# One product-key expert step, two layers: the planned order of selection, gathered rows and one-hots

## The chip, the core and the metric

The kernel runs on one core of a Trainium2 chip. The metric is the device time of one execution in microseconds (us). TensorE (PE), VectorE (DVE), ScalarE (ACT), GpSimd (POOL) and SyncE (SP) each run their own queue in order; the queues meet at semaphores. A transfer (DMA) is issued from the queue of SP, ACT or POOL.

## The reference, cut to what matters

Two trunk layers over 640 tokens (128 context, 512 latent; five blocks of 128). Each layer has a mixer and then an expert retrieval, `peer`. The mixers and the norms are not touched here.

```python
def peer(h, w_q, sub_keys, u_tab, v_tab):             # T = 640 tokens, D = 1024
    q = (x @ w_q).reshape(T, 8, 2, 128)               # 8 heads, two sides
    scores = einsum('thsd,hskd->thsk', q, sub_keys)   # 128 keys a side
    s, i = top_k(scores, 16)                          # per side
    cand = s[:, :, 0, :, None] + s[:, :, 1, None, :]  # 16 x 16 sums
    top, sel = top_k(cand, 16); idx = take(i0 * 128 + i1, sel)
    g = softmax(top)                                  # 16 experts of 16384 for each head and token
    a = gelu(einsum('td,thkd->thk', x, u_tab[idx]))
    return einsum('thk,thkd->td', g * a, v_tab[idx])
```

## The kernel before

The expert step of a layer has three stretches. The first two share one planned order; the third follows it.

**Two ways to an expert's output.** For the first two blocks of tokens ("gathered blocks", `GB = 2`) the rows of both tables are fetched by index: a gather moves 128 rows of 4 KB, one for each token. A "dot" (L1484) multiplies a gathered u row with the token and sums it; an "add" (L1519) adds a gathered v row, weighted, to the result. There are `ROWS` = 256 dots and 256 adds; a dot and an add together are called a pair here. For the other three blocks ("dense blocks", `DB = 3`) all 16384 experts are computed: PE multiplies every u row with every token in 128 u jobs (a few tokens, 32 of the third block, go by 32 extra gathered dots, "qdots", L1494), the chosen gates are scattered into a dense gate matrix, and PE multiplies the product with the whole v table (the value stretch). Gates are scattered by matmuls of one-hots: a "hot" is four tokens' one-hots, made by DVE (L1531, L1533) and partly by ACT (the "build" steps), and a scatter is PE's four matmuls of it. There are 96 hots and 96 scatters in a layer.

**Selection.** For each head (`PHEADS = 8`) PE computes two q jobs and five scores (one for each block); DVE then does five "choose" blocks (eight parts each, L1391 to L1419) and a "batch" (13 parts) which turns the picks of all five blocks into indices and gates. Part 0 of the batch subtracts the maximum and lets ACT compute the exponentials; part 10 writes the gathered rows' indices (L1460), releases the gathers and then waits for ACT's exponentials (L1468); parts 11 and 12 finish the gates.

**The order.** `dve_order` writes DVE's queue by hand: the whole first head, then dots from 0 on, each followed (from dot `LAG` = 20 on) by the add that is 20 behind it, and after each of these as much of the remaining work (chooses, batches, hots, qdots: `rest`, by the guessed costs in `CHOOSE`, `BATCH` and beside the kinds) as `each` has paid for. `each` is the cost of all remaining work over `EARLY * TOPK` = 160 pairs. When the rest is done, "weigh" steps (L1560, L1561: gate times activation for one of 32 chunks of the value stretch) follow among the remaining pairs. POOL walks the same list and issues the gathers; each table has a ring of `RING` = 4 buffers, so a gather waits for the dot or add four before it.

`peer_steps_of` writes PE's and ACT's common order: a walk over `dve_order` with a planned clock (1.03 times the guessed cost, from 20 us on) gives a due time for each score, exponential, build and scatter (3 us behind the hot it needs), and the jobs are laid out with what is due put between them, by `COST` (8.9 us for a q job, 4.95 for a u job). The last `LATE` = 4 jobs are kept back until every scatter is placed. DVE may be at most `OHB` = 4 hots ahead of PE's scatters. u weights are loaded two jobs at a time into four slots (`peer_jobs`, `peer_weights`).

**End of the second stretch.** After the last scatter ACT copies it out and stores the last gates to memory (L1158); then SP loads gates for the first chunks (1.5 MB, strided); then DVE weighs chunk 0 and PE starts on the values.

Of the kernel before, what the change touches and what calls it, by code (L numbers as in the profile page):

```python
# [8 lines left out]
BF16 = mybir.dt.bfloat16  # L9
# [55 lines left out]
EARLY = 10  # L65
SPREAD = 28
LATE = 4
# [76 lines left out]
def program(nc, x_in, cond_t, norm_gain, final_gain, ada_w, ada_b, ada_fix_in, ab_w_in, ab_w_out, decays, states,  # L144
# [3 lines left out]
    with ctx:  # L148
# [93 lines left out]
        pair, side_h, which = (bcf[:, 3328 + i * 80:3408 + i * 80].bitcast(BF16).rearrange("p (k c) -> p k c", c=SIDES) for i in range(3))  # L242
# [38 lines left out]
        part_i = small[:, 1360:1520].rearrange("p (k b s) -> p b s k", b=BLOCKS, s=2)  # L281
# [136 lines left out]
        def peer_jobs(l):  # L418

            loads, jobs = [], []  # L420

            def load_of(kind, c, n):
                loads.append((kind, c, len(jobs) + n))
                jobs.extend((kind, c * n + i, len(loads) - 1) for i in range(n))

            for c in range(CHUNKS):
                for q in [n for n, at in enumerate((0, 0, 2, 2, 6, 6, 10, 10)) if at == c]:
                    load_of("q", q, 2)
                for half in range(2):
                    load_of("u", 2 * c + half, 2)  # L430
            return loads, jobs

        CHOOSE = (.58, 1.47, .56, 1.2, .27, .65, .27, .34)
        BATCH = (1.2, .75, .25, 1.5, 1.5, .8, .45, .3, .25, .6, .4, .1, .4)

        def dve_order():

            picks = []
            for h in range(PHEADS):
                picks += [("choose", h, b, i, w) for b in range(BLOCKS) for i, w in enumerate(CHOOSE)]  # L440
                picks += [("batch", h, 0, i, w) for i, w in enumerate(BATCH)]
# [7 lines left out]
            first = len(CHOOSE) * BLOCKS + len(BATCH)  # L449
            order, rest = picks[:first], picks[first:]  # L450
            each, due, pairs, weighed = sum(p[4] for p in rest) / int(EARLY * TOPK), 0.0, 0, 0
            for i in range(ROWS + LAG):
# [6 lines left out]
                due += each  # L459
# [10 lines left out]
        COST = {"q": 8.9, "u": 5.4 * DU / DT}  # L470

        def peer_steps_of(jobs):

            ready, clock, begun = [], 20.0, [0.0] * SCORE_LEAD
            for kind, a, b, i, w in dve_order():
# [5 lines left out]
                clock += 1.03 * w  # L481
# [4 lines left out]
                if kind == "batch" and a == PHEADS - 1 and i == len(BATCH) - 1:  # L486
                    ready += [(clock + 1, "turn", b, 0) for b in ORDER[:-1]]
                    ready += [(clock + 1, "build", ORDER[0], g) for g in range(OHB - 2)]
# [4 lines left out]
                if kind == "hot":  # L493
# [3 lines left out]
                    ready.append((clock + 3, "scatter", a, b))  # L497
# [549 lines left out]
        def _(act):  # L1047
# [49 lines left out]
            def peer(l):  # L1097
# [63 lines left out]
                for kind, a, i in steps:  # L1161
                    if kind == "job":
                        take_job(a)
                    elif kind == "exp":
                        act.wait_ge(top_ready, l * PHEADS + a + 1)
                        f(top_e, top_e, ACT.Exp).then_inc(exp_ready, 1)
# [110 lines left out]
        def _(v):  # L1277
# [101 lines left out]
            def peer(l):  # L1379
# [41 lines left out]
                def batch(h, part):  # L1421
# [4 lines left out]
                    top = top_i.rearrange("p b k -> p (b k)")  # L1426
                    of = lambda t: t.rearrange("p (b k) -> p b k", b=BLOCKS)
                    to = pair.rearrange("p k (b s) -> p b s k", s=2)
                    wide4 = onehot.rearrange("p (a k c) -> p a k c", a=TOPK, k=TOPK)
                    if part == 0:  # L1430
                        v.wait_ge(scores_read, l * BLOCKS * PHEADS + (h + 1) * BLOCKS)
                        v.tensor_tensor(top_e, top_v, top_v[:, :, 0:1].to_broadcast([P, BLOCKS, TOPK]), ALU.subtract)\
                            .then_inc(top_ready, 1)
                        for t, n, op in ((by16, 4, ALU.logical_shift_right), (by4, 2, ALU.logical_shift_right),
                                         (mid2, 12, ALU.bitwise_and), (low2, 3, ALU.bitwise_and)):
                            own.mark(v.tensor_scalar(t, top, n, None, op))
                    elif part == 1:
                        own.mark(v.scalar_tensor_tensor(out=to[:, :, 0, :], in0=of(by4), scalar=float(WIDE * TOPK // NARROW - WIDE),
                                                        in1=of(by16), op0=ALU.subtract, op1=ALU.max))
                        own.mark(v.scalar_tensor_tensor(out=off, in0=top, scalar=float(WIDE * TOPK), in1=mid2, op0=ALU.is_lt, op1=ALU.mult))  # L1440
                        own.mark(v.tensor_copy(side_h.rearrange("p k c -> p (k c)"), small[:, 960:1120].bitcast(U32)))
                    elif part == 2:
                        own.mark(v.tensor_tensor(to[:, :, 1, :], of(off), of(low2), ALU.add))
                    elif part == 3:
                        own.mark(v.tensor_tensor(wide4, pair.unsqueeze(1).to_broadcast([P, TOPK, TOPK, SIDES]),
                                                 which.unsqueeze(2).to_broadcast([P, TOPK, TOPK, SIDES]), ALU.is_equal))
                    elif part == 4:
                        own.mark(v.tensor_tensor(wide4, wide4, side_h.unsqueeze(2).to_broadcast([P, TOPK, TOPK, SIDES]), ALU.mult))
                    elif part <= 8:
                        n = NP * (8 >> part - 5)  # L1450
                        out = onehot[:, 0:n] if part < 8 else small[:, 1360:1520]
                        own.mark(v.tensor_tensor(out, onehot[:, 0:n], onehot[:, n:2 * n], ALU.add))
                    elif part == 9:
                        own.mark(v.tensor_copy(ijg[:, :, 0:2, at], part_i[:, GB:BLOCKS, :, :]))
                        own.mark(v.scalar_tensor_tensor(out=part_i[:, 0:GB, 0, :], in0=part_i[:, 0:GB, 0, :], scalar=float(NKEYS),
                                                        in1=part_i[:, 0:GB, 1, :], op0=ALU.mult, op1=ALU.add))
# [415 lines left out]
```

## Time and profile before

| | us |
|---|---|
| median of 3 runs (4048.28 to 4056.04) | 4049.79 |
| the profiled execution | 4056.96 |
| its span, first to last instruction | 4055.1 |
| layer 0: first q job to last scatter | 555.84 to 1444.7 |
| layer 0: value stretch | 1469.58 to 2131.0 |
| layer 1: first q job, start of values | 2470.22, 3379.93 |

PE is busy for 3866.5 us of the span (95%), DVE for 2628.7 (65%), POOL for 1447.8 (36%), ACT for 688.7 (17%). Times in the views are counted from the first instruction. Matmuls overlap, so the length of a PE piece is read from its start to the start of the next. A matmul of 32-bit numbers shows as two records: a u job is 16 records, a q job 32, a scatter 8, a score 4.

### The profile page before, as it was taken

The numbers are of one execution on the slowest core, as the hardware profiler recorded it, in microseconds if no ns is written. First come the engines' busy times: TensorE is split into PE (matmuls) and PEld (weight loads), VectorE is DVE, ScalarE is ACT, GpSimd is POOL, SyncE is SP. The second block draws the span as 40 slices with busy tenths as digits, with TensorE's granted clock in tenths as the row PEclk, the third lists the DMA queues.
The fourth block names the chain that finished last, engine by engine and source line by source line (L and its number), as shares of the span: only waits on it lengthen the run. The fifth ranks groups of instructions, "written<-read, shape, count | busy, mean of one in ns | idle before, by whom it ended". The sixth has DMA issues, their size and how long they took to land.

```text
span 4055.1 us, 36430 instructions
## 1 busy us (share of the span) xinstructions
PE 3866.5 (95%) x12776; PEld 2211.7 (55%) x12776; DVE 2628.7 (65%) x5808; ACT 688.7 (17%) x1591; POOL 1447.8 (36%) x1180
## 2 busy tenths in 40 slices
PE   8999889999988989999998999999999899999998
PEld 1555556666656744444445545666666674444443
DVE  2682558998777955454445944998977894445444
ACT  1111011111334620000001221111143460000000
POOL 0110003554556634444320000455545663434331
PEclk9999899999989999999999999999999999999999
DMA  9452037999999999999972101899999999999994
GB/s 333 160 195 83 8 128 286 331 334 342 342 379 396 405 365 353 341 355 358 329 259 83 42 31 46 313 333 325 343 351 384 410 404 345 363 352 345 352 326 168
DMA packets 377653, 1155.57 MB, mean 285 GB/s; under 512 B 28720, under 2 KB 163360, under 8 KB 346360
## 3 DMA queue, kind: packets, MB, share of 16 engines
q0 software_dynamic: 170016, 618.96, 41.5%
q1 hardware_dynamic: 198368, 483.93, 32.7%
q10 hardware_dynamic: 9088, 50.37, 3.0%
q8 instruction: 102, 1.67, 0.2%
q14 instruction: 79, 0.65, 0.0%
HBM read 1055.68 MB, written 97.40 MB: 284 GB/s over the span
## 4 chain that ended last, share of the span: by engine, by line
PE 75%; DMA 10%; DVE 10%; POOL 3%; issue 1%; ACT 1%; SPq 0%; DVEq 0%; POOLq 0%
PE bank L744 74%; DMA ring<-in_peer_v,work 4%; POOL ring L696 3%; DMA ring<-in_peer_u,q_t 3%; DVE diag L1519 2%; DVE ring L1484 1%; DVE bc L1533 1%; DMA ring<-in_peer_u,work 1%; DVE bc L1531 1%; DVE ring L1651 1%; DMA bc<-peer_gates 1%; DMA ring<-in_ada_w 1%; DVE ring L1494 0%; DMA peer_gates<-work 0%; ACT hT L1050 0%
## 5 line engine op out<-in xcount | busy, mean ns | idle before, releaser
L744 PE MATMUL bank<-hT,ring 128*128 128x352 f32 (+3 forms) x5696 | 1691.8, 456 | 3.3 <-ACT hT L1050 3.3
L744 PEld LDWEIGHTS bank<-hT,ring 128*128 128x128 f32 x5696 | 1058.7, 193 | 560.7 <-issue 83.0
L696 POOL DMA_INDIRECT ring<-in_peer_u,work x512 | 753.3, 1471 | 1360.2 <-DVE ring L1484 1075.0
L744 PE MATMUL bank<-ring,work 128*128 128x512 f32 x2016 | 868.8, 592 | 0.0
L1519 DVE SCALAR_TENSOR_TENSOR diag<-ring,work,diag 128x1024 f32<-128x1024 f32 x508 | 652.5, 1285 | 96.5 <-DMA ring<-in_peer_v,work 84.4
L696 POOL DMA_INDIRECT ring<-in_peer_v,work x512 | 557.2, 1088 | 296.0 <-issue 155.2
L1484 DVE SCALAR_TENSOR_TENSOR ring<-ring,work 128x1024 f32<-128x1024 f32 x512 | 623.9, 1219 | 49.2 <-DMA ring<-in_peer_u,work 48.9
L744 PEld LDWEIGHTS bank<-ring,work 128*128 128x128 f32 x2016 | 383.0, 190 | 482.2 <-issue 482.2
L1050 ACT ACTIVATE work<-bank 128x352 f32<-128x352 f32 (+3 forms) x528 | 274.6, 522 | 1560.3 <-PE bank L744 1513.9
L744 PE MATMUL bank<-work 128*128 128x512 f32 x1056 | 461.4, 597 | 9.7 <-DVE work L1561 9.7
L1560 DVE COPY work<-bc 128x128 f32<-128x128 f32 x64 | 14.5, 227 | 663.7 <-DMA work<-peer_acts 443.7
L744 PE MATMUL bank<-ring,hT 128*128 128x384 f32 (+1 forms) x960 | 353.4, 525 | 8.5 <-ACT hT L1050 8.5
L744 PEld LDWEIGHTS bank<-work 128*128 128x128 f32 x1056 | 202.2, 192 | 265.2 <-issue 265.2
L744 PE MATMUL bank<-bc 128*128 128x128 f32 x1536 | 211.6, 288 | 74.1 <-DVE bc L1533 65.7
L744 PEld LDWEIGHTS bank<-ring,hT 128*128 128x128 f32 x960 | 180.3, 191 | 171.3 <-issue 83.9
L744 PEld LDWEIGHTS bank<-bc 128*128 128x128 f32 x1536 | 199.2, 200 | 107.9 <-DVE bc L1533 78.6
L1050 ACT ACTIVATE work<-work 128x16 f32<-128x16 f32 (+3 forms) x49 | 14.2, 304 | 1115.1 <-DVE ring L1484 1102.3
L1050 ACT ACTIVATE bc<-work,small 128x128 f32<-128x128 f32 x352 | 152.8, 483 | 0.0
L1788 DVE SCALAR_TENSOR_TENSOR work<-work,small 128x670 f32<-128x670 f32 x180 | 149.4, 905 | 0.0
L1533 DVE TENSOR_TENSOR bc<-small,keep 128x512 f32<-128x512 f32 x192 | 130.3, 679 | 0.0
L1531 DVE TENSOR_SCALAR bc<-keep,small 128x128 f32<-128x128 f32 x416 | 122.2, 340 | 11.7 <-ACT small L1050 10.8
L744 PE MATMUL bank<-ring,stat 128*2 128x512 f32 x240 | 107.7, 603 | 15.4 <-DMA ring<-in_ada_w 15.4
(178 smaller groups left out, 2077.1 us busy)
## 6 DMA issues: line engine op xcount, KB each, us to landing
ring<-in_peer_ut SPq DMA_DIRECT2D x128, 1024.0 KB, 8.4
ring<-in_peer_vt SPq DMA_DIRECT2D x42, 2048.0 KB, 9.9
peer_gates<-work ACTq DMA_DIRECT2D x48, 1024.0 KB, 8.7
bc<-peer_gates SPq DMA_DIRECT2D x32, 1536.0 KB, 22.3
work<-in_peer_vt SPq DMA_DIRECT2D x22, 2048.0 KB, 10.3
peer_acts<-work SPq DMA_DIRECT2D x60, 704.0 KB, 6.3
work<-peer_acts SPq DMA_DIRECT2D x60, 704.0 KB, 13.9
ring<-in_ada_w SPq DMA_DIRECT2D x12, 2048.0 KB, 14.4
```

The costliest lines, as they stand in the source:

```text
L696: nc.gpsimd.indirect_dma_start(row, None, table, bass.IndirectOffsetOnAxis(ap=at, axis=0)).then_inc(s, 16)
L744: return nc.tensor.matmul(out, lhsT, rhs, start=start, stop=stop, **kw)
L1050: return nc.scalar.activation(out, in_, func, **kw)
L1484: v.scalar_tensor_tensor(out=row, in0=row, scalar=1.0, in1=h_tok[:, n % GB, :], op0=ALU.mult, op1=ALU.mult, accum_out=dots[:, n % 2, k:k + ...
L1519: v.scalar_tensor_tensor(out=a, in0=row, scalar=wgt[:, n % 2, k:k + 1], in1=a, op0=ALU.mult, op1=ALU.add).then_inc(v_free, 1)
L1531: v.tensor_scalar(oh[:, n % OHB, 0, o, :], iota, ijg_t[:, b, 0, t0 + o:t0 + o + 1], ijg_t[:, b, 2, t0 + o:t0 + o + 1], ALU.is_equal, ALU.mult)
L1533: v.tensor_tensor(oh[:, n % OHB, 1, :, :], ijg_t[:, b, 1, t0:t0 + OH].unsqueeze(2).to_broadcast([P, OH, NKEYS]), iota.unsqueeze(1).to_broa ...
L1560: v.tensor_copy(w[:, :, 0:skip, :], g[:, :, 0:skip, :])
L1651: ins = v.scalar_tensor_tensor(out=a, in0=w, scalar=by, in1=a, op0=ALU.mult, op1=ALU.add)
L1788: ins = v.scalar_tensor_tensor(out=y_conv[:, f, :], in0=src, scalar=w, in1=y_conv[:, f, :], op0=ALU.mult, op1=ALU.add)
```

## The change

Rates, paces and a split of the first head; no engine gets another kind of work.

- `EARLY = 10` for all remaining work becomes two rates: selection is paid over 6.25 x 16 = 100 pairs and the hots and qdots over 3 x 16 = 48.
- `GROUPS`: the first head is selected in two groups, first the two gathered blocks alone and later the three dense ones; the other heads in one group as before. So there are nine batches; `batch` works on blocks b0 to b1 and writes gathered indices only in groups that hold the gathered blocks.
- The last three parts of a batch (sum of the exponentials, reciprocal, gates) become `share`, which follows the first choose block of the next group.
- The planned order of PE and ACT uses other paces (0.957 during selection, 1.1 after), other job costs, scatters 8 us behind their hot instead of 3, `LATE` = 6, and scores of the first head one job earlier. The q weights are loaded a half chunk apart.

```diff
-EARLY = 10
+EARLY_CHOICE, EARLY = 6.25, 9.25
-LATE = 4
+LATE = 6
+BEHIND = 8
+PACE = {True: 0.957, False: 1.1}
+BEGIN = 20.0
...
-                for q in [n for n, at in enumerate((0, 0, 2, 2, 6, 6, 10, 10)) if at == c]:
-                    load_of("q", q, 2)
                 for half in range(2):
+                    for q in [n for n, at in enumerate((0, 1, 4, 5, 12, 13, 20, 21)) if at == 2 * c + half]:
+                        load_of("q", q, 2)
                     load_of("u", 2 * c + half, 2)
...
-        BATCH = (1.2, .75, .25, 1.5, 1.5, .8, .45, .3, .25, .6, .4, .1, .4)
+        BATCH = (1.2, .75, .25, 1.5, 1.5, .8, .45, .3, .25, .6, .4)
+        SHARE = (.25, .2, .4)
+        GROUPS = [(0, 0, GB), (0, GB, BLOCKS)] + [(h, 0, BLOCKS) for h in range(1, PHEADS)]
+        NG = len(GROUPS)
...
-            for h in range(PHEADS):
-                picks += [("choose", h, b, i, w) for b in range(BLOCKS) for i, w in enumerate(CHOOSE)]
-                picks += [("batch", h, 0, i, w) for i, w in enumerate(BATCH)]
+            shared = lambda s: [("share", s, 0, i, w) for i, w in enumerate(SHARE)]
+            for s, (h, b0, b1) in enumerate(GROUPS):
+                for b in range(b0, b1):
+                    picks += [("choose", h, b, i, w) for i, w in enumerate(CHOOSE)]
+                    if s and b == b0:
+                        picks += shared(s - 1)
+                picks += [("batch", s, 0, i, w * (.3 + .7 * (b1 - b0) / BLOCKS)) for i, w in enumerate(BATCH)]
+            picks += shared(NG - 1)
...
-            first = len(CHOOSE) * BLOCKS + len(BATCH)
+            first = len(CHOOSE) * GB + len(BATCH)
             order, rest = picks[:first], picks[first:]
-            each, due, pairs, weighed = sum(p[4] for p in rest) / int(EARLY * TOPK), 0.0, 0, 0
+            work = lambda kinds: sum(p[4] for p in rest if p[0] in kinds)
+            chosen, placed = work(("choose", "batch", "share")), work(("hot", "qdot", "qweight"))
+            choice_rate, hot_rate = chosen / (EARLY_CHOICE * TOPK), placed / ((EARLY - EARLY_CHOICE) * TOPK)
...
-                due += each
+                due += (choice_rate if rest and rest[0][0] in ("choose", "batch", "share") else hot_rate)
...
-        COST = {"q": 8.9, "u": 5.4 * DU / DT}
+        COST = {"q": 9.15, "u": 5.16 * DU / DT}
...
-                clock += 1.03 * w
+                choosing = choosing and kind != "hot"
+                clock += PACE[choosing] * w
...
-                    ready.append((clock + 3, "scatter", a, b))
+                    ready.append((clock + BEHIND, "scatter", a, b))
...
-                return ready[0][1] != "score" or q_at[2 * ready[0][2] + 1] + 2 <= n
+                return ready[0][1] != "score" or q_at[2 * ready[0][2] + 1] + (2 if ready[0][2] else 1) <= n
...
-                    now += {"score": .6, "turn": .5, "scatter": 1.1}.get(step[0], 0)
+                    now += {"score": .45, "turn": .5, "scatter": 1.08}.get(step[0], 0)
...
-                        v.wait_ge(exp_ready, l * PHEADS + h + 1)
-                        own.mark(v.tensor_reduce(top_s, top_e, AX.X, ALU.add))
+                def share(s, part):
+                    if part == 0:
+                        v.wait_ge(exp_ready, l * NG + s + 1)
+                        own.mark(v.tensor_reduce(top_s[:, b0:b1], top_e[:, b0:b1], AX.X, ALU.add))
```

## Rows read from the trace of the kernel before

**Rows 1.** Chain of waits, end of layer 0's second stretch: start us, us, what.

```profile
1442.65 2.09 PE bank L744 x8
...
1445.38 7.37 DMA peer_gates<-work
1452.83 14.64 DMA bc<-peer_gates
...
1469.58 661.42 PE bank L744 x1536
```

**Rows 2.** Busy time by stretch: selection, one-hots in two parts, values; layer 1's first one-hot part.

```profile
core 0: us, PE busy (x) PEld busy (x) DVE busy (x) ACT busy (x) POOL busy (x), PEclk, DMA share, GB/s
555.80:1063.30 507.50, 507.46 (x1856) 341.03 (x1857) 424.67 (x1496) 69.63 (x119) 223.89 (x178) 1.00 0.81 297
...
1085.70:1292.90 207.20, 181.38 (x736) 125.38 (x735) 154.03 (x262) 77.09 (x202) 124.23 (x99) 0.93 0.99 391
1292.90:1441.90 149.00, 138.55 (x722) 105.39 (x720) 137.06 (x275) 99.43 (x261) 94.05 (x63) 0.98 1.01 404
1469.60:2131.00 661.40, 661.38 (x1536) 292.49 (x1536) 306.17 (x371) 5.89 (x14) 245.88 (x203) 1.00 0.92 332
...
3000.40:3206.80 206.40, 180.31 (x736) 124.96 (x735) 153.96 (x262) 76.78 (x202) 118.88 (x101) 0.93 1.00 399
```

**Rows 3.** PE's waits from 1060 to 1480: who waited for whom, us, times, longest.

```profile
PE bank L744 <- DVE bc L1533: 33.5, 15, 4.9
PE bank L744 <- DVE work L1561: 5.1, 1, 5.1
```

**Rows 4.** PE in order of time: start us, us, instructions, idle before.

```profile
585.00 8.78 PE L744 MATMUL bank<-hT,ring 128*128 128x320 f32 x32
593.62 0.61 PE L744 MATMUL bank<-bc,work 128*128 128x128 f32 x4
594.06 4.90 PE L744 MATMUL bank<-hT,ring 128*128 128x352 f32 x16
...
1135.15 1.05 PE L744 MATMUL bank<-bc 128*128 128x128 f32 x8
1136.04 4.90 PE L744 MATMUL bank<-hT,ring 128*128 128x352 f32 x16
1140.77 1.05 PE L744 MATMUL bank<-bc 128*128 128x128 f32 x8
...
1313.33 1.95 PE L744 MATMUL bank<-bc 128*128 128x128 f32 x16
...
1316.41 4.90 PE L744 MATMUL bank<-hT,ring 128*128 128x352 f32 x16
...
1433.28 1.13 PE L744 MATMUL bank<-bc 128*128 128x128 f32 x8 [0.70 <-issue]
1435.12 1.13 PE L744 MATMUL bank<-bc 128*128 128x128 f32 x8 [0.70 <-DVE bc L1533]
```

**Rows 5.** DVE's groups, 555.8 to 1469.6: shapes, count | busy us, mean ns | idle before.

```profile
L1484 DVE SCALAR_TENSOR_TENSOR ring<-ring,work 128x1024 f32<-128x1024 f32 x165 | 201.1, 1219 | 23.4 <-DMA ring<-in_peer_u,work 23.3
L1519 DVE SCALAR_TENSOR_TENSOR diag<-ring,work,diag 128x1024 f32<-128x1024 f32 x143 | 183.1, 1281 | 35.9 <-DMA ring<-in_peer_v,work 33.0 <-issue 2.4
```

**Rows 6.** Waits from 624 to 1060, DVE for the exponentials.

```profile
DVE small L1468 <- ACT small L1050: 32.6, 5, 9.5
```

**Rows 7.** DMA queues from 1085.7 to 1292.9, the gathers': packets, MB, share.

```profile
q0 software_dynamic: 14056, 51.16, 64.1%
```

**Rows 8.** Waits from 1470 to 2160, DVE before its weigh steps.

```profile
DVE work L1560 <- DMA work<-peer_acts: 231.2, 15, 17.1
DVE work L1560 <- PE bank L744: 79.8, 15, 14.4
```

**Rows 9.** POOL in order of time, first gather of layer 0.

```profile
614.96 1.01 POOL L696 DMA_INDIRECT ring<-in_peer_u,work  x1 [83.97 <-DVE work L1460]
```

**Rows 10.** The hots' L1533 alone in one-hot part 1: length, DVE busy and count.

```profile
1085.70:1292.90 207.20, 21.80 (x32) 0.93 0.99 391
```

More of the change, by code:

```diff
@@ L241, in program @@
         onehot = bcf[:, 2048:2048 + TOPK * NP // 2].bitcast(BF16)
-        pair, side_h, which = (bcf[:, 3328 + i * 80:3408 + i * 80].bitcast(BF16).rearrange("p (k c) -> p k c", c=SIDES) for i in range(3))
+        pair, side_h, which = (bcf[:, 3328 + i * 80:3408 + i * 80].bitcast(BF16) for i in range(3))
         by16, by4, low2, mid2, off = (bcf[:, 3568 + i * 80:3648 + i * 80].bitcast(U32) for i in range(5))
@@ L485, in peer_steps_of @@
                     ready.append((clock + 3, "gelu", a // TOPK, 0))
-                if kind == "batch" and a == PHEADS - 1 and i == len(BATCH) - 1:
+                if kind == "share" and a == NG - 1 and i == len(SHARE) - 1:
                     ready += [(clock + 1, "turn", b, 0) for b in ORDER[:-1]]
@@ L1419, in choose, with batch @@
                         own.mark(v.max_index(top_i[:, b, 8:16], top_v[:, b, 8:16], cand_left))
-                def batch(h, part):
+                def batch(s, part):
+                    h, b0, b1 = GROUPS[s]
+                    n, lo, heads_c = b1 - b0, GB - b0, 2 * (b1 - b0)
                     at = slice(h * TOPK, (h + 1) * TOPK)
@@ L1444, in batch @@
                     elif part == 3:
-                        own.mark(v.tensor_tensor(wide4, pair.unsqueeze(1).to_broadcast([P, TOPK, TOPK, SIDES]),
-                                                 which.unsqueeze(2).to_broadcast([P, TOPK, TOPK, SIDES]), ALU.is_equal))
+                        own.mark(v.tensor_tensor(wide4, in_rows(pair).unsqueeze(1).to_broadcast(wide_shape),
+                                                 which.rearrange("p (k c) -> p k c", c=SIDES)[:, :, 0:heads_c].unsqueeze(2).to_broadcast(wide_shape),
+                                                 ALU.is_equal))
@@ L1447, in batch @@
                     elif part == 4:
-                        own.mark(v.tensor_tensor(wide4, wide4, side_h.unsqueeze(2).to_broadcast([P, TOPK, TOPK, SIDES]), ALU.mult))
+                        own.mark(v.tensor_tensor(wide4, wide4, in_rows(side_h).unsqueeze(2).to_broadcast(wide_shape), ALU.mult))
                     elif part <= 8:
-                        n = NP * (8 >> part - 5)
-                        out = onehot[:, 0:n] if part < 8 else small[:, 1360:1520]
-                        own.mark(v.tensor_tensor(out, onehot[:, 0:n], onehot[:, n:2 * n], ALU.add))
+                        m = TOPK * heads_c * (8 >> part - 5)
@@ L1453, in batch @@
+                        out = onehot[:, 0:m] if part < 8 else part_i[:, 0:m]
+                        own.mark(v.tensor_tensor(out, onehot[:, 0:m], onehot[:, m:2 * m], ALU.add))
                     elif part == 9:
-                        own.mark(v.tensor_copy(ijg[:, :, 0:2, at], part_i[:, GB:BLOCKS, :, :]))
-                        own.mark(v.scalar_tensor_tensor(out=part_i[:, 0:GB, 0, :], in0=part_i[:, 0:GB, 0, :], scalar=float(NKEYS),
-                                                        in1=part_i[:, 0:GB, 1, :], op0=ALU.mult, op1=ALU.add))
@@ L1578, in peer @@
                 v.wait_ge(h_ready[2 * l + 1], BLOCKS)
-                own.mark(v.tensor_copy(which, iota[:, 0:TOPK].unsqueeze(2).to_broadcast([P, TOPK, SIDES])))
+                own.mark(v.tensor_copy(which.rearrange("p (k c) -> p k c", c=SIDES), iota[:, 0:TOPK].unsqueeze(2).to_broadcast([P, TOPK, SIDES])))
                 for kind, a, b, i, _ in dve_order():
@@ L1584, in peer @@
                         batch(a, i)
+                    elif kind == "share":
+                        share(a, i)
                     elif kind == "hot":
```

86 lines of the change are left out of this document (54 added, 32 removed).

## The prediction

> **What bounds the kernel now.** I read the busy times by stretch first, then the chain of waits, then who made PE wait, then PE in order of time. In layer 0 selection keeps PE busy for 507.46 of 507.5 us at full clock, and the value stretch for 661.38 of 661.4 [rows 2]: there the time is PE's own work. Only the one-hots leave a gap. In their first part, the 32 hots that carry the qdots [rows 10], PE is busy for 181.4 of 207.2 us at a granted clock of 0.93, and the DMA engines are full: 391 GB/s, 399 in layer 1, 404 in the part after [rows 2]. PE waits 33.5 us for DVE's hots [rows 3], and DVE for rows, 23.3 and 33.0 us [rows 5]. So the chain there is: gathers, dots and adds, the hot queued behind them on DVE, the scatter. At the end comes a tail: last scatter from 1442.65, gates stored 7.37, gates loaded 14.64, weigh, values from 1469.58 [rows 1]. The four jobs kept back cover it all but 5.1 us [rows 3].
>
> What PE would need without waits is a sum. From start to start a u job takes 4.73, a scatter 0.89, a q job 8.62, a score 0.44 [rows 4]. Selection before: 74 u, 16 q and 40 scores, 350.0 + 137.9 + 17.6 = 505.5; measured 507.5, so 2.0 for the start. All of it (128 u, 16 q, 40 scores, 96 scatters, three transposes of 0.45) is 847.7 + 2.0 = 849.7 us. From 555.84 to 1469.58 it took 913.7. The 64 us between the two are all that a better order can win in a layer.
>
> **The change, part by part.** The order is worked out from the formulas. Before, one rate paid for everything: 427.8 of guessed cost over 160 pairs, 2.67 a pair. Now selection gets 272.4 over 100 (2.72) and hots and qdots 181.4 over 48 (3.78). The first hot then stands behind dot 101 (93 before), the ninth behind 104 (98), the 41st behind 127 (131), the last behind 149 (161). So the hots have 48 pairs among them instead of 68, and 12 pairs go to the value stretch; selection takes 8 more.
>
> *Selection* costs PE nothing that I can find. DVE was busy for 424.7 us there [rows 2]. Eight more dots at 1.22 and adds at 1.28 [rows 5] are 20 us; the second batch of head 0 repeats some fifteen short instructions, 3 us estimated. The first score is done 18 us after PE's start (two q jobs and no third), at 574.6, so DVE ends near 574.6 + 448 + 10 (the first gather on its way) = 1033. PE asks for the gates when its sum reaches the transposes: now 75 u jobs stand ahead, 512.3 us, so 1068; I add 2 for the first score, which waits for ACT to take its q job, and for an exponential now and then at which ACT waits for DVE with jobs queued behind: 1070. There are 37 us to spare; even if DVE still waited the 32.6 us for exponentials [rows 6] that `share` should take off, 4 would be left. That saving and the earlier first gather (POOL waited 84 us for it [rows 9]) are therefore worth 0 by themselves: PE hides them. Moved q loads: every job still finds two loads ahead of it; 0.
>
> *One-hots, first eight.* Two u jobs now stand ahead of the first scatter. The ninth hot needs the fifth scatter done (four buffers): two transposes, four u jobs, five scatters, 24.3 us, so it starts at 1094 (1085.7 before).
>
> *One-hots with qdots.* From the 9th to the 41st hot there were 33 dots, 32 qdots and 33 adds, 98 gathers of 0.52 MB: the queue's 51.16 MB [rows 7]. Now it is 23, 32 and 23: 78, 40.7 MB. The other traffic was 81.0 - 51.2 = 29.8 MB; with 27 u jobs for 29 and the same 32 scatters I take 28. At 391 GB/s 68.7 MB take 176 us. PE's own sum here is 27 x 4.73 + 32 x 0.89 = 156, so DMA still sets the end, by less than before. Bounds: if the gathers alone count, 207.2 x 78/98 = 165; if nothing but PE does, 156; if a hot costs as much as now, 207. I take 176: bytes over a rate that three rows show within 4%. The 41st hot starts at 1270; its scatter ends at 1272.
>
> The Trainium skill (DMA: Bandwidth & Descriptors, Specifications) gives some 358 GB/s as a core's memory limit and 435 as the fabric's ceiling. By 358 this part would take 192 us and the sum lose 16 us a layer; the 391, 399 and 404 measured here are above it, so it is no limit in this trace. By 435 it would take 158, which is the first rival; no stretch read here holds that rate.
>
> *The other one-hots.* DVE was busy for 137.1 of 149 us [rows 2]; eight pairs fewer at 2.50 leave 117. PE needs 15 u jobs, 55 scatters and a transpose: 120.4. Three scatters in a row take 3.08, not 2.67, and the last run goes at 1.84 apiece [rows 4]; nine threes, a four and a run of 14 ahead of the last jobs (10 before) add 3.7 + 1 + 13.3. That is 138 us, and PE bounds it now: last scatter done at 1411.
>
> *The tail.* Six jobs are kept back: 28.4 us, over the tail's 24.9 (1444.7 to 1469.6 [rows 1]). So the 5.1 us wait goes; ACT's take of the last job costs about 1. Values start at 1440, where they started at 1469.6: 29.5 us. In layer 1 the first part was served at 399 GB/s, so it needs 172 us; that layer went from first job to values in 909.7 us and now in 881: 29.
>
> *Value stretch.* Twelve pairs more: 30 us of DVE, which was busy for 306 of 661 [rows 2] and waited 79.8 us for PE and 231 for stored activations [rows 8]; they go into that idle time. 12.5 MB more make 351 GB/s of 332, below what the one-hots carried. I cost it at 0. Were that cover gone, it would be 12.5 MB at 332 GB/s, 38 us a layer.
>
> **The sum**: the profiled execution took 4056.96, less 58 gives 3999. It lies 7.2 above the median of the runs, so the forecast for the median is 3991.
>
> **The rivals.** First, *PE alone*: DVE may run four hots ahead, DMA holds a rate nearer its peaks, and the qdot part fits into PE's 156 us. Then the 41st scatter ends 14 us earlier: 44 us a layer, 3963. For it speaks that four hots, some 19 us at PE's pace, nearly cover the 20 us by which the gathers are late; against it that 68.7 MB in 156 us are 440 GB/s, and no stretch read here went above 404.
>
> Second, *half the gain*: scatters are planned 1.1 times DVE's guessed cost and 8 us behind, and the qdot part is planned at 162 us where I expect 176. If latency and not bytes holds the u gathers (a gather waits for the dot four before), or a PE wait lowers the clock as it did (0.93 [rows 2]), 190 us are possible: 14 us less in each layer, 4020.
>
> Third, *nothing comes of it*: the 32 hots still take 207 us, since qdots, not pairs, hold DVE. The sum is then 31 us a layer worse and the time 4050 to 4055. Against it: 20 of 98 gathers are gone.
>
> Fourth, *slower*: the value stretch pays. If weighs there come after gathers that no longer land in time, PE waits in the one stretch where it never did. It decides from the point where a weigh is later than the product before it, so more than 20 us of lead have to go; its price is the 38 us above, against 29 won: 9 us a layer lost, 4068. The Trainium skill's 358 GB/s (DMA: Bandwidth & Descriptors, Specifications) would be nearly reached by 351, yet not passed, so by that rule too the stretch stays as it is. Against it speaks that DVE waits for PE there already [rows 8].
>
> That the change does not do what it says (the gates late, so the transposes wait at 1070) needs DVE to lose 37 us in selection; I count it with the third.
>
> **How the numbers follow.** My case 0.58 (3978 to 4008), PE alone 0.16, half 0.13, nothing 0.06, slower 0.07. A difference of 0.2% (8 us) is about what a measurement of this kernel can tell. Faster by more: 0.58 + 0.16 + 0.13 = 0.87; within: 0.06; slower: 0.07. The range takes in the first three: 3955 to 4032.
>
> **What would show it.** The first transposes at about 1070 with no wait of PE before them; the 41st hot near 1270, with 170 to 180 us for the 32 before it at 385 to 405 GB/s; PE's waits for DVE (33.5 us [rows 3]) down to about half; the last scatter near 1411, then six jobs and values with under 1.5 us between; the value stretch still 661 us. DVE's wait for exponentials gone, and no gain to be seen from it before 1063. Wrong would be: PE idle in selection, ACT waiting for DVE for more than one job's 4.7 us, or a value stretch over 665 us.

## The result, and the profile after

The changed kernel takes 3988 us where the kernel before, timed beside it, takes 4051: a ratio of 0.9835 (95% interval 0.9821 to 0.9849), 63 us less. The forecast was 3991, within 3955 to 4032. The profiled execution took 3988.73 us with a span of 3986.9, which is 68.2 less than the span before.

The busy times by stretch answer [rows 2]: selection, the one-hots with qdots (9th to 41st hot), the other one-hots, the values of layer 0, then the qdot part of layer 1. Columns: stretch, length, busy time of each engine with its instructions, granted clock, DMA share, GB/s.

```profile
553.50:1068.10 514.60, 513.71 (x1872) 344.70 (x1873) 445.32 (x1538) 72.97 (x124) 243.15 (x193) 0.99 0.86 310
1092.90:1269.60 176.70, 166.53 (x724) 116.57 (x722) 129.78 (x231) 78.89 (x200) 89.65 (x78) 0.99 0.99 387
1269.60:1401.30 131.70, 122.95 (x683) 95.84 (x683) 118.44 (x251) 97.85 (x256) 62.84 (x46) 1.00 0.99 386
1433.85:2093.30 659.45, 659.45 (x1536) 291.76 (x1536) 339.80 (x409) 6.11 (x15) 277.39 (x227) 1.00 0.95 351
2971.30:3144.30 173.00, 164.29 (x712) 114.99 (x711) 129.75 (x231) 78.93 (x200) 93.67 (x79) 0.99 1.00 390
```

The qdot part went from 207.2 to 176.7 us and from 206.4 to 173.0, with the DMA engines as full as before; the rest of the one-hots from 149.0 to 131.7. The value stretch carries 351 GB/s where it carried 332, and PE is busy through all of it.

From the first job to the values, both kernels in layer 0 (first the kernel before, from 555.8):

```profile
555.80:1469.60 913.80, 871.32 (x3498) 602.78 (x3498) 749.26 (x2090) 265.86 (x634) 462.78 (x354) 0.98 0.89 337
```

```profile
553.50:1433.85 880.35, 859.22 (x3497) 595.37 (x3497) 722.30 (x2069) 271.86 (x636) 414.13 (x330) 0.99 0.90 336
```

The 33.45 us gained in this layer are 21.35 us of idle PE (42.48 before, 21.13 now) and 12.1 us by which the same PE work got shorter (871.3 to 859.2). The last section shows that most of the 12.1 is PE's clock.

PE's waits for DVE's hots answer [rows 3]; here from 1060 to 1440 (who waited for whom, us, times, longest). They went from 33.5 to 14.8 us, and the wait for the first weigh (5.1 us) is gone.

```profile
PE bank L759 <- DVE bc L1573: 14.8, 11, 4.8
PE bank L759 <- issue: 2.6, 3, 1.2
PE bank L759 <- ACT work L1065: 2.1, 3, 0.8
```

The end of the second stretch answers [rows 1] (PE in order of time: start, us, instructions, idle before). Behind the last scatter stand six jobs (96 records), then the values with 0.55 us between.

```profile
1402.08 1.99 PE L759 MATMUL bank<-bc 128*128 128x128 f32 x8 [1.43 <-DVE bc L1573]
1403.87 29.43 PE L759 MATMUL bank<-hT,ring 128*128 128x352 f32 x96
1433.85 6.70 PE L759 MATMUL bank<-work 128*128 128x512 f32 x15 [0.55 <-ACT work L1065]
```

Two executions had a lower granted clock and are not compared: one of the changed kernel (5332.9 us, mean clock 0.718) and the profiled one of the kernel with `LATE` 4 (4642.2 us, 0.826).

Where the span's 68.2 us went: 2.4 ahead of layer 0's first job, 33.4 from there to its values (913.7 to 880.4), 1.5 from there to layer 1's first job, 28.3 in layer 1 (909.7 to 881.4), 2.6 behind it. 61.7 of them lie in the two planned stretches. The 1.5 and the 2.6 come from the value stretches, which are 1.9 and 2.5 us shorter (661.4 and 662.0 before, 659.5 now in both layers). Before, PE waited 5.1 and 4.6 us for the first weigh, and the values then began at about half the clock; now they begin at the full one. The rows are the first 4.4 us of layer 0's values before, then their first 6.1 us now:

```profile
1469.60:1474.00 4.40, 4.40 (x6) 1.98 (x7) 1.39 (x1) 0.00 (x0) 0.00 (x0) 0.55 0.98 417
```

```profile
1433.90:1440.00 6.10, 6.10 (x15) 2.75 (x16) 1.69 (x2) 0.00 (x0) 0.00 (x0) 1.00 0.95 336
```

### The profile page after: what moved, and what is told of

It is laid out like the page before. It is cut to its first block, busy times and chain, and to the rows that moved or that the text cites. A ratio compares the mean times of both kernels' runs of the same rounds, so it can differ in the third digit from the quotient of the medians.

```text
span 3986.9 us, 36490 instructions
## 1 busy us (share of the span) xinstructions
PE 3840.1 (96%) x12776; PEld 2195.3 (55%) x12776; DVE 2642.8 (66%) x5842; ACT 701.6 (18%) x1597; POOL 1413.5 (35%) x1180
## 4 chain that ended last, share of the span: by engine, by line
PE 84%; DVE 7%; DMA 7%; ACT 1%; issue 1%; POOL 1%; ACTq 0%; DVEq 0%; SPq 0%
PE bank L759 83%; DMA ring<-in_peer_u,q_t 3%; DMA ring<-in_peer_v,work 2%; DVE ring L1693 1%; DMA ring<-in_peer_u,work 1%; DVE diag L1559 1%; DVE ring L1534 1%; DVE bc L1573 1%; DMA ring<-in_ada_w 1%; POOL ring L711 1%; DVE ring L1524 1%; DVE bc L1571 0%; DMA peer_gates<-work 0%; ACT work L1065 0%; ACT hT L1065 0%
## 5 line engine op out<-in xcount | busy, mean ns | idle before, releaser
L711 POOL DMA_INDIRECT ring<-in_peer_u,work x512 | 730.3, 1426 | 1339.5 <-DVE ring L1524 1042.3
L759 PE MATMUL bank<-bc 128*128 128x128 f32 x1536 | 197.9, 281 | 38.4 <-DVE bc L1573 27.6
L759 PEld LDWEIGHTS bank<-bc 128*128 128x128 f32 x1536 | 190.7, 195 | 65.6 <-DVE bc L1573 40.0
L1065 ACT ACTIVATE work<-keep,small 128x128 f32<-128x128 f32 x352 | 120.8, 393 | 30.8 <-PE bank L759 14.2
## 6 DMA issues: line engine op xcount, KB each, us to landing
ring<-in_ada_w SPq DMA_DIRECT2D x12, 2048.0 KB, 14.4
```

The source lines that it names most:

```text
L711: nc.gpsimd.indirect_dma_start(row, None, table, bass.IndirectOffsetOnAxis(ap=at, axis=0)).then_inc(s, 16)
L759: return nc.tensor.matmul(out, lhsT, rhs, start=start, stop=stop, **kw)
L1065: return nc.scalar.activation(out, in_, func, **kw)
```

## The experiments

Between sessions one kernel's time moves by more than within one. The changed kernel was timed again beside the last three kernels:

> The changed kernel itself, unaltered, timed beside the next three. Theory and rivals alike expect 3988 us within 12, and a ratio to the kernel before of 0.9835 within 0.003. It tells whether the 3977 to 3979 us of the two kernels without the split and with the shares beside their loads differ from it.

It took 3975.6 us (3969.1 to 3978.2), 12.8 less than in the first session. Its ratio to the kernel before is 0.9823 (0.9809 to 0.9836), and it agrees with the first. So kernels timed in different sessions are compared below by their ratios, and by stretches of their traces. The traces of one kernel differ too: the second one of the changed kernel has 876.1 and 870.3 us from first job to values, where the first has 880.4 and 881.4. A difference of up to some 10 us a layer between two traces is therefore not a finding by itself.

**The pairs put back, the rest of the change kept.**

```diff
-EARLY_CHOICE, EARLY = 6.25, 9.25
+EARLY_CHOICE, EARLY = 6.25, 10.5
-PACE = {True: 0.957, False: 1.1}
+PACE = {True: 0.957, False: .95}
```

> The changed kernel with 20 pairs put back among the hots (68 instead of 48) and the planner's pace set so that PE's order around the scatters is the same to the step where it matters. Theory: 98 gathers and 27 u jobs between the 9th and the 41st hot, 79 MB, 203 us at 391 GB/s instead of 177; the rest as slow as before (147 us); values start about 922 us after the first q job, and the time is 4060 to 4080, no better than before. Rival (the new selection and the new paces give the gain): at most 4020.

With 68 pairs a pace of 0.95 gives PE nearly the order that 1.1 gives with 48: no scatter moves past more than one job, and six jobs follow the last. It took 4066.6 us, a ratio of 1.0035 (1.0021 to 1.0050). The qdot part is back at its old length (first row, columns as above), and PE waits 42.8 us for hots. From first job to values it takes 921.9 and 919.8 us.

```profile
1091.30:1298.70 207.40, 176.97 (x722) 122.80 (x720) 154.13 (x263) 80.90 (x204) 123.33 (x98) 0.92 0.99 381
...
PE bank L759 <- DVE bc L1573: 42.8, 16, 6.9
```

The gain hangs on the pairs: without them the split, the shares and the changed plan give nothing.

**The rates alone**, put into the kernel before; PE's order is planned from them by the old paces.

```diff
-EARLY = 10
+EARLY_CHOICE, EARLY = 5.8125, 8.8125
...
-            each, due, pairs, weighed = sum(p[4] for p in rest) / int(EARLY * TOPK), 0.0, 0, 0
+            work = lambda kinds: sum(p[4] for p in rest if p[0] in kinds)
+            chosen, placed = work(("choose", "batch")), work(("hot", "qdot", "qweight"))
+            choice_rate, hot_rate = chosen / (EARLY_CHOICE * TOPK), placed / ((EARLY - EARLY_CHOICE) * TOPK)
+            due, pairs, weighed = 0.0, 0, 0
...
-                due += each
+                due += (choice_rate if rest and rest[0][0] in ("choose", "batch") else hot_rate)
```

> The kernel before with nothing changed but the two rates: selection over 93 pairs as it was, hots and qdots over 48. No split of the first head, no share, the old paces, LATE 4. Theory (the gain is the gathers taken out of the one-hots): the 9th to the 41st hot hold 80 gathers (41.8 MB) and 24 u jobs, some 68 MB, so 173 us at 391 GB/s instead of 207; values start about 885 us after the first q job (913.7 before, 880.4 changed), and the time is about 3995 (3985 to 4005). Rival (the split of the first head, the share parts and the paces carry it): 4030 or more.

It took 4027.9 us, a ratio of 0.9945 (0.9926 to 0.9963). That is a miss of the theory, and close to its rival's 4030. What the theory said of DVE holds: the qdot part took 176.2 and 173.1 us, and the last scatter was done 850.1 us after the first job (850.6 in the changed kernel). But eleven jobs stand behind that scatter:

```profile
1400.68 1.13 PE L747 MATMUL bank<-bc 128*128 128x128 f32 x8 [0.17 <-issue]
1401.65 52.23 PE L747 MATMUL bank<-hT,ring 128*128 128x352 f32 x176
1454.44 5.85 PE L747 MATMUL bank<-work 128*128 128x512 f32 x13 [0.55 <-ACT work L1053]
...
PE bank L747 <- DVE bc L1536: 21.7, 12, 5.1
PE bank L747 <- issue: 8.9, 19, 2.1
```

The old plan counts on hots earlier than they come, so PE stood at its scatters with jobs behind them that it could have done. 52 us of jobs, where the tail needs some 25 to 30, put the values 902.7 us after the first job in place of 880.4. DVE's shorter queue is worth its full price only with an order of PE that fits it. All waits listed for PE around the one-hots come to 33.6 us here and to 20.1 in the changed kernel, which is some 13 of these 22 us. PE's own work is 10 us longer (869.2 for 859.2); the clock, worked out as in the last section, is 7 of them.

**The pace alone**, with the changed pairs.

```diff
-PACE = {True: 0.957, False: 1.1}
+PACE = {True: 0.957, False: .95}
```

> The changed kernel with one number other: the planned pace of the hots 0.95 instead of 1.1, so that PE's order puts the 41st scatter 24 us earlier in PE's own sum (677 us after the first job instead of 701) and 11 instead of 6 u jobs behind the last scatter. Theory (the second half of the gain is that PE has jobs to do while DVE waits for rows): DVE's hots come when they came, 41st about 716 us and last about 848 us after the first job, PE waits for them with the jobs still ahead of it, and 11 jobs follow: values at about 901 us instead of 880, 20 us a layer, 4028 (4018 to 4036). Rival (the order of PE does not matter as long as DVE sets the end; what the run with the rates alone lacked was the split, share or LATE): 3988 within 10.

It took 4009.0 us, a ratio of 0.9905 (0.9889 to 0.9922), which is under the theory's band. The direction holds, and the size is smaller than the 40 us that were expected: 28 or 33 us by the ratios (0.9835 and 0.9823 for the changed kernel). From first job to values it takes 890.6 and 891.6 us, 10.2 more in each layer than in the first trace of the changed kernel, and 14.5 and 21.3 more than in the second. Again eleven jobs follow the last scatter, but in layer 0 this scatter comes 12.6 us sooner than in the first trace (838.0 us after the first job). The expectation held the hots' times fixed, and they came sooner: 3.0 us of the 12.6 lie ahead of the qdot part, 6.5 in it and 3.1 behind it. The row of the qdot part, then the u weights' queue (packets, MB, share) in it, here and in the changed kernel:

```profile
1090.90:1261.10 170.20, 147.79 (x639) 105.02 (x638) 129.07 (x232) 77.23 (x197) 93.23 (x80) 0.94 0.99 380
```

```profile
q1 hardware_dynamic: 2448, 15.86, 22.3%
```

```profile
q1 hardware_dynamic: 3024, 19.73, 27.4%
```

With jobs moved out of the part their weights go too: 64.7 MB in place of 68.4. At the changed kernel's 387 GB/s they would take 167 us, and they took 170.2. That the length is bytes over rate stands; the bytes are a choice of the order as well.

**Bytes or latency.** A u load brings the weights of two jobs. From the 45th load on only the first job's weights are loaded, and the second job multiplies what its half of the slot held before (the activations are then not the reference's); every gather stays.

```diff
-                        sp.dma_start(load_slot[n % 4], peer_ut[l, c // 2][:, c % 2 * 2048:(c % 2 + 1) * 2048]).then_inc(load_in[n % 4], 16)
+                        cols = 1024 if c >= 44 else 2048
+                        sp.dma_start(load_slot[n % 4][:, 0:cols], peer_ut[l, c // 2][:, c % 2 * 2048:c % 2 * 2048 + cols]).then_inc(load_in[n % 4], 16)
```

> The changed kernel with only half of the bytes of each u load from the 45th load of u on (the second job of a load multiplies what its half of the slot held before), so the activations are not the reference's; every step and every wait stays. Theory (bytes over a rate bound the hots with qdots): 68.4 MB become 61, 158 us at 387 GB/s, which is PE's own 156; values start some 16 us earlier in each layer, 3957 (3945 to 3965). Rival (the ring: a u gather waits for the dot four before it, so 55 u gathers at 3.2 us each): 174 us or more as before and at most 8 us gained in all, 3980 or more.

It took 3957.2 us, a ratio of 0.9768 (0.9751 to 0.9784). The qdot part carries 61.5 MB in place of 68.4 and takes 162.1 us, with the same 32 hots and the same gathers, and PE is now busy through all of it:

```profile
1094.70:1256.80 162.10, 161.97 (x715) 114.60 (x714) 129.07 (x232) 78.73 (x200) 94.87 (x78) 1.00 0.99 379
...
PE bank L760 <- DVE bc L1574: 3.3, 3, 1.4
```

So bytes set the end in the changed kernel, and not the four buffers of a ring at a fixed time for each gather, with which the rival's 174 us or more would have stayed. The gathers did land sooner with fewer bytes beside them (those of the qdots after 9.4 us at the median, for 10.9), so a landing time that grows with the load is part of the same limit and is not told apart from it here.

**The split of the first head, and the shares.** Each is undone alone.

```diff
-        GROUPS = [(0, 0, GB), (0, GB, BLOCKS)] + [(h, 0, BLOCKS) for h in range(1, PHEADS)]
+        GROUPS = [(h, 0, BLOCKS) for h in range(PHEADS)]
...
-            first = len(CHOOSE) * GB + len(BATCH)
+            first = len(CHOOSE) * BLOCKS + len(BATCH)
```

> The changed kernel with the first head selected in one group again. Theory (PE hides the earlier first gather): no change from the changed kernel, 3988, within 6 us. Rival (selection on DVE needs the earlier start to be done by the transposes): DVE is done some 13 us after the point where PE asks, in each layer, and the time is 4005 to 4015.

```diff
-                    if s and b == b0:
-                        picks += shared(s - 1)
...
-            picks += shared(NG - 1)
+                picks += shared(s)
...
-            first = len(CHOOSE) * GB + len(BATCH)
+            first = len(CHOOSE) * GB + len(BATCH) + len(SHARE)
```

> The changed kernel with the share parts straight behind their batch. Theory (4 us would be left even with the waits for exponentials): 3988, within 6 us. Rival: in the changed kernel DVE was done with selection only 6.5 us before PE asked for the transposes, so 10 to 25 us more of waits push the transposes back by up to 20 us a layer: 4000 to 4025.

They took 3977.3 us, a ratio of 0.9814 (0.9794 to 0.9835), and 3979.1 us, a ratio of 0.9821 (0.9801 to 0.9842). The changed kernel's two ratios are 0.9835 and 0.9823. Neither part is worth anything that these runs can tell. With the shares at once DVE waits 33.0 us for exponentials in selection, and PE does not notice: its first transposes come at 1067.9 us, 514.6 after the first job as in the changed kernel.

```profile
DVE small L1502 <- ACT small L1063: 33.0, 7, 8.1
```

**Fewer jobs kept back.**

```diff
-LATE = 6
+LATE = 4
```

> The changed kernel with four jobs planned behind the last scatter in place of its six; nothing else of PE's order moves by more than two places. Theory: the stretch from the last scatter to the values is set by the last products (24.9 us after the last scatter before the change, 29.8 behind it), four jobs fill 18.9 us of it, PE then stands some 6 us each layer and the stretch is 25 us in place of 29.8; the two jobs taken away lie earlier, where PE waits 14.8 us for one-hots, and take some of that: within 10 us of the changed kernel. Rival: what follows the last scatter is pure addition, and each job taken from there gains its 4.7 us, twice a layer: 19 us less, 3969.

It took 3985.2 us, a ratio of 0.9842 (0.9827 to 0.9857), beside 3975.6 and 0.9823 of the changed kernel on the same chip: 10 us more. The two ranges (3982.1 to 3988.8, and 3969.1 to 3978.2) do not overlap, while the intervals of the ratios do. The rival's 19 us less are excluded; the jobs behind the last scatter do cover a tail. That PE's wait before the values is where the 10 us sit was expected, but no trace that can be compared shows it.

**More pairs to the values: 8, 16 and 32.** The first has only the rate changed, `EARLY` 8.75; the second has

```diff
-EARLY_CHOICE, EARLY = 6.25, 9.25
+EARLY_CHOICE, EARLY = 6.25, 8.25
-PACE = {True: 0.957, False: 1.1}
+PACE = {True: 0.957, False: 1.2}
```

> The changed kernel with hots and qdots over 40 pairs instead of 48 (8 pairs more in the value stretch). By the theory of bytes the 9th to the 41st hot hold 72 gathers and 25 u jobs, 64 MB, 166 us; the long run of scatters at the end is gone from PE's order; 7 jobs follow the last scatter: values start 10 to 17 us earlier in each layer, 3955 to 3970, and the value stretch stays at 659.5 us with some 364 GB/s. Rival (the value stretch pays for them): 8.4 MB at 351 GB/s, 24 us a layer, 4000 or more.

> The changed kernel with hots and qdots over 32 pairs (16 more in the value stretch) and the planned pace of the hots 1.2, so that 6 jobs follow the last scatter. By the theory 62 gathers and 25 u jobs, 59 MB, 152 us: less than PE's own sum there, so PE alone bounds the one-hots; values start about 855 us after the first job, 25 us earlier in each layer, 3938 (3930 to 3950), with the value stretch at 659.5 us and about 376 GB/s. Rival (the value stretch pays): 16.8 MB at 351 GB/s, 48 us a layer, 4020 or more; between them if the lead of the weighs runs out only in part of the stretch.

They took 3968.5 us, a ratio of 0.9797 (0.9781 to 0.9814), and 3943.3 us, a ratio of 0.9738 (0.9722 to 0.9754). Both times lie in the theory's bands. The qdot part takes 160.8 and 149.7 us, the value stretch 659.5 in both. The first is not clear of the changed kernel: its interval overlaps that of the ratio 0.9823, and its values start 873.8 and 874.2 us after the first job, where 10 to 17 us of gain were expected and the changed kernel's second trace has 876.1 and 870.3. The second is clear of both of the changed kernel's ratios; its values start after 860.9 and 854.1 us. The third kernel is the second with the first head in one group, as in the diff on `GROUPS` above:

> The kernel with 16 pairs more in the values' stretch and hot pace 1.2 (3943 us), with head 0's gathered blocks in one group again. Theory: the group of its own is worth nothing, since VectorE has 19 us or more to spare in the selection: 3943 within 8. Rival: with fewer pairs to gather the head's indices are wanted as early as they can be had, and one group for all makes the first chunk 12 us or more later: 3955 to 3970.

It took 3933.5 us (3930.5 to 3937.8), a ratio of 0.9722 (0.9707 to 0.9737). That is 1.5 us under the theory's band and far from the rival's; its interval overlaps that of the kernel with the split, so the two can't be told apart, but it is the simplest of the faster ones and has the lowest time here, 115 us under the kernel before. First job to values, layer 0:

```profile
551.70:1405.00 853.30, 851.79 (x3498) 592.49 (x3498) 682.71 (x2003) 266.89 (x632) 374.86 (x298) 1.00 0.88 327
1087.00:1236.70 149.70, 149.70 (x676) 106.98 (x676) 113.05 (x211) 79.00 (x203) 74.80 (x65) 1.00 0.99 392
```

PE idles for 1.5 us of 853.3, at a full granted clock; the sum of PE's own work was put at 849.7 in the prediction. So hardly anything is left to win ahead of the values by a better order of the same work.

Last, `EARLY` 7.25 with pace 1.35, and the first head split as in the changed kernel:

> The changed kernel with 32 pairs more in the values' stretch and hot pace 1.35. It looks for the point from which the values' stretch pays for the pairs that it takes: it must then carry (351 x 659 + 32 x 0.75 MB x 1000) / 659 = about 388 GB/s for all of its 659 us, against 351 in the changed kernel, and the leads of its rows before PE, 16 us at the least with 16 pairs more, run out. Theory: the one-hots were bound by PE already with 16 pairs more, so nothing is left to gain ahead of the values, and the stretch grows past 659.5 us: 3945 to 4000, slower than the kernel with 16 pairs more (3943). Rival: the stretch carries it, and the fewer jobs and gathers ahead leave the time where it is: 3925 to 3945.

It took 3987.0 us, a ratio of 0.9843 (0.9828 to 0.9858), 53 us more than the kernel with 16 pairs more and one group, on the same chip. From first job to values it takes 854.0 and 854.3 us, nearly as there (853.3 and 852.2); the value stretch took 686.6 and 684.2 us in place of 659.5, which both kernels with 16 pairs more have. First its stretch and three pieces of it, then PE's waits in it; below, two of the same pieces with 16 pairs more:

```profile
1411.20:2100.00 688.80, 668.86 (x1536) 293.91 (x1536) 422.87 (x512) 6.54 (x17) 356.07 (x293) 0.99 1.01 387
1550.00:1700.00 150.00, 150.00 (x351) 66.46 (x350) 87.40 (x113) 0.43 (x2) 82.19 (x63) 1.00 1.03 400
1700.00:1850.00 150.00, 143.71 (x324) 62.67 (x323) 99.36 (x123) 0.43 (x2) 86.39 (x70) 0.97 1.03 399
1850.00:2000.00 150.00, 142.28 (x327) 62.28 (x326) 92.58 (x116) 0.43 (x2) 80.95 (x70) 0.99 1.03 398
...
PE bank L759 <- DMA ring<-in_peer_vt: 10.2, 4, 3.7
PE bank L759 <- DMA work<-in_peer_vt: 7.4, 2, 3.7
```

```profile
1405.00:2064.50 659.50, 659.43 (x1536) 291.72 (x1536) 379.24 (x458) 6.32 (x16) 310.69 (x259) 1.00 0.99 376
1700.00:1850.00 150.00, 150.00 (x351) 66.41 (x350) 86.04 (x107) 0.43 (x2) 72.94 (x61) 1.00 1.03 400
1850.00:2000.00 150.00, 150.00 (x351) 66.42 (x350) 90.29 (x108) 0.43 (x2) 72.08 (x60) 1.00 1.03 394
```

The DMA engines run at 394 to 400 GB/s in these pieces of both; with 16 pairs more the v weights still come in time, with 32 they don't. The price is 27 and 25 us a layer. PE's waits there are for the v weights (17.6 us; 2.2 us of the window lie behind the stretch); the rest of the 27 is 9.4 us of longer PE work, at a granted clock of 0.97 and 0.99 in the last two pieces. The weighs never came late, but their lead (from the end of a weigh to the product that reads it, with the stretch divided evenly among its 32 chunks) was as good as gone: 29 us at the least before the change once the first chunks are past, 25 in the changed kernel, 16 or 17 with 16 pairs more, 0 to 2 with 32.

## Why the prediction was right, and where it was not

**Selection.** First transposes 514.6 us after the first job, for 514 forecast; PE loses nothing there. DVE was busy for 445.3 us, for 448. Wrong was when DVE ends: at 1061.8, not 1033, 6 us before PE wants the gates and not 37. The forecast gave DVE 10 us of waiting, and from its first score (at 575.4) to its last gates it stood idle for 43.6: 21.0 for exponentials, 7.6 for scores, 4.5 for rows, the rest in short gaps. So its wait for exponentials did not go, though the forecast named the end of this wait as a sign; of 32.6 us [rows 6] 21.0 are left, and no gain was counted on them (who waited for whom in selection, us, times, longest; then DVE around the longest):

```profile
DVE small L1504 <- ACT small L1065: 21.0, 4, 11.6
...
1049.27 0.17 DVE L1490 TENSOR_SCALAR q_t<-q_t 128x16 uint32<-128x16 f32 x1
1061.03 0.24 DVE L1504 TENSOR_REDUCE small<-small 128x5 f32<-128x80 f32 x1 [11.58 <-ACT small L1065]
```

The last group has no next group, so its share stands straight behind its batch, and ACT serves it behind jobs. The slack was thinner than forecast, yet it held. Of the signs of being wrong none came: PE idles for 0.9 us in selection, no wait of ACT for DVE is listed there, and the value stretch stays under 665 us.

**The first gather.** POOL waits 60.7 us for it and not 84 [rows 9]; as forecast, nothing came of it, as the kernel without the split shows.

```profile
589.28 1.01 POOL L711 DMA_INDIRECT ring<-in_peer_u,work  x1 [60.66 <-DVE work L1488]
```

**One-hots with qdots.** Forecast 176 and 172 us from 68.7 MB; measured 176.7 and 173.0 with 68.44 MB, in layer 0, of which the gathers' queue, answering [rows 7], is (packets, MB, share)

```profile
q0 software_dynamic: 11029, 40.20, 59.9%
```

for 40.7 forecast. Bytes over a rate that the stretch itself had shown was the right rule, and the kernel with half the u bytes shows it. PE alone (the first rival) would have needed those bytes away; a fixed latency of the rings (in the second) is excluded.

**The other one-hots and the tail.** The last scatter was done 850.6 us after the first job, for 855 forecast. The surplus for scatters in runs was sized 6.7 us too high: three in a row took 2.67 us and not 3.08, the four 3.57, and the last run of 14 took 23.8 us and not 25.8. The 41st hot started 2 us later than forecast, which took some of that back. The 1.84 us for a scatter of the last run is not PE's own work either: rows 4 show 0.70 us of idle PE in it, and in the changed kernel PE stands for 8.2 of the 23.8 us. Six jobs then cover the tail but for 0.55 us. The values start at 880.4 and 881.4 us, for 884 and 881.

**Value stretch.** It was costed at 0, and it took 659.5 us for 661.4 before, at the forecast 351 GB/s; the 1.9 us are the clock at its start. DVE's wait for PE, the cover that was named, answers [rows 8]: from 79.8 us to

```profile
DVE work L1600 <- DMA work<-peer_acts: 207.6, 15, 16.6
...
DVE work L1600 <- PE bank L759: 9.5, 1, 9.5
```

So that cover was used up by 12 pairs, and yet 16 more cost nothing: DVE's idle time moved but its weighs still came in time. The fourth rival's point was put at a lead of 20 us used up by weighs. The runs put it between 16 and 32 pairs beyond the change, with the v weights late first, while the DMA engines carry 398 to 400 GB/s at a share of 1.03.

**The sum.** The forecast took 58 us from the profiled execution, and the span lost 68.2: 61.7 in the stretches that the steps cover (33.4 for 29.5, 28.3 for 29), 4.4 in the value stretches and about 2 in code that the change doesn't touch. The 4.4 were put at nothing, since the forecast counted the wait for the first weigh but not the clock behind it. Between the medians it is 63 us. That the layers came out within 4 us of the sum is in part luck: the second trace of the same kernel has gains of 37.6 and 39.4 us for the same 29.5 and 29.

**What the prediction did not say.** It took the plan's paces, `BEHIND` and `LATE` as given and gave them no term of their own. They are not nothing: with the rates alone 24 us of 63 come about (4052.2 to 4027.9), and a pace of 0.95 in place of 1.1 takes 28 to 33 us. Also of the 33.45 us in layer 0 a third was no wait but shorter PE work, at a granted clock of 0.99 in the qdot part for 0.93 before; the sum met that because it went by PE's own durations at full clock and by bytes.

**Still open** is where the 10 us of the kernel with `LATE` 4 sit, and why two traces of the changed kernel differ by 4.3 and 11.1 us in the planned stretches.

## What to carry to other kernels

When DMA is full and an in-order producer hands its results to an in-order consumer, count the bytes that each piece of work brings into the stretch: the length is bytes over the rate that this stretch has shown, and it follows both from the gathers taken out and from the loads whose jobs are moved out. Change the producer's order and the consumer's plan together, since with the old plan the shorter queue brought 24 of its 63 us. Move work under the next stretch until the DMA engines carry there what they carried at their fullest, and look at the weights of the covering stretch as well as at the lead of its products: here 16 pairs more were free and 32 cost 52 us.

## What the runs showed of the hardware

Stretches with gathers of 4 KB rows and loads of 1 and 2 MB together ran at 376 to 404 GB/s in the rows above with a DMA share of 0.98 to 1.03, over 130 to 690 us on end, and at 413 GB/s in one part of 144 us (the second part of the kernel with the pairs put back, share 1.02). The Trainium skill (DMA: Bandwidth & Descriptors, Bandwidth) has single-core measurements up to 425 GB/s with the other core of the pair idle and about 358 with both streaming; this trace agrees with the first, and with one core at work the prediction's weighing of 358 as a limit was beside the point.

```profile
1298.70:1442.80 144.10, 130.26 (x678) 102.08 (x679) 137.13 (x276) 100.51 (x259) 88.95 (x63) 0.92 1.02 413
```

The granted clock, a mean over a stretch between PE's levels of 1.2 and 2.4 GHz (0.5 and 1), fell with PE's waits for hots in layer 0's one-hots: it was 0.92 in the qdot part with 42.8 us of waits, 0.93 with 33.5 [rows 2, 3], 0.94 with 23.3, 0.95 with 21.7 (the rates alone), 0.99 with 14.8, 1.00 with none. Here PE in the kernel before, around one wait of 4.86 us, and the 5 us behind it, with the clock at 0.50:

```profile
1120.74 1.16 PE L744 MATMUL bank<-bc 128*128 128x128 f32 x8 [1.59 <-DVE bc L1533]
1126.76 2.07 PE L744 MATMUL bank<-bc 128*128 128x128 f32 x8 [4.86 <-DVE bc L1533]
1128.63 6.68 PE L744 MATMUL bank<-hT,ring 128*128 128x352 f32 x16
1135.15 1.05 PE L744 MATMUL bank<-bc 128*128 128x128 f32 x8
...
1126.80:1131.80 5.00, 5.00 (x14) 3.75 (x15) 5.00 (x9) 0.60 (x1) 4.09 (x4) 0.50 0.91 321
```

From start to start this scatter took 1.87 us where one takes 0.89 at the full clock, and the u job, partly at the lower level, 6.52 where one takes 4.73 [rows 4]. From the transposes to the values of layer 0 the clock stood at the lower level for 40.4 us before the change, with PE busy in 28.8 of them, and for 6.8 us (6.3 busy) after it. Work takes twice as long there, as the scatter shows, so half of the busy time is lost: 14.4 and 3.2 us, a difference of 11 of the 12.1 us by which the PE work got shorter. From first job to values the same PE work took 871.3, 869.2, 863.3, 859.2 and 851.8 us with 33.5, 21.7, 23.3, 14.8 and no waits for hots (before; the rates alone, which has 8.9 us of other short waits; the pace alone; the changed kernel; the fastest kernel), so a wait cost more here than its own length.
